# Memory projections in halves of 256 columns: the key half of both token tiles first, then the value half

## The reference, cut to what matters

```python
def memory_attention(q, mem, mem_norm_g, w_mem_kv, q_norm_g, k_norm_g):
    kv = rms_norm(mem, mem_norm_g) @ w_mem_kv            # (256, 1024) @ (1024, 512)
    k, v = jnp.split(kv.reshape(B, M, 2 * MEM_HEADS, HEAD_DIM), 2, axis=2)
    q = rms_norm(q, q_norm_g)
    k = rms_norm(k, k_norm_g)
    logits = jnp.einsum('bshd,bmhd->bhsm', q, k).astype(jnp.float32) * (HEAD_DIM ** -0.5)
    p = jax.nn.softmax(logits, axis=-1)
    out = jnp.einsum('bhsm,bmhd->bshd', p.astype(v.dtype), v)

for i in range(DEPTH):                                   # DEPTH = 2
    if i == 1: k_shared, v_shared = ...                  # from h @ w_kv
    h = swiglu_half_step(h, ffn1_norm[i], ffn1_w_gate_up[i], ffn1_w_down[i])
    z = rms_norm(h, mix_norm[i]) @ w_in[i]               # 1024 -> 1024
    y_mix = pool mixer (i = 0) or banded attention (i = 1) of z[..., :768]
    y_mem = memory_attention(z[..., 768:], mem, ...)
    h = h + concatenate([y_mix, y_mem]) @ w_out[i]
    h = swiglu_half_step(h, ffn2_norm[i], ffn2_w_gate_up[i], ffn2_w_down[i])
```

## Time and profile before

| | us |
|---|---|
| time, median of 3 runs | 980.77 (980.74 to 981.02) |
| span of the profiled execution, first to last instruction | 977.7 |
| PE busy | 949.3 (97%) |
| DVE busy | 554.0 (57%) |
| ACT busy | 457.7 (47%) |
| POOL busy | 50.0 (5%) |
| DMA queue of the weights | 164.65 MB, 50.6% of 16 engines' span |

### The profile page before, as it was taken

The page is one execution under the profiler, slowest core; times in us unless marked ns, Lnnn a source line. Parts: engine busy times, 40 slices in busy tenths (PEclk is TensorE's granted clock), DMA queues, the critical chain, the costliest instruction groups (busy, mean ns, idle before and its releaser), DMA issues.

```text
span 977.7 us, 12400 instructions
## 1 busy us (share of the span) xinstructions
PE 949.3 (97%) x4515; PEld 779.0 (80%) x4515; DVE 554.0 (57%) x650; ACT 457.7 (47%) x642; POOL 50.0 (5%) x85
## 2 busy tenths in 40 slices
PE   7999999999999999999899999999998999999998
PEld 5888888887777888888688888888876878888886
DVE  5655454674557455555676546455776565455552
ACT  6544444444435443444545434353556455353441
POOL 3300000010000000000210000000130000000000
PEclk9999999999999999999999999999999999999999
DMA  9966556364145746464366555652740246646442
GB/s 318 293 220 202 184 183 203 129 237 161 42 150 193 250 149 212 157 214 172 108 215 215 187 199 173 213 169 103 266 129 1 86 164 212 217 152 209 163 129 86
DMA packets 121054, 172.74 MB, mean 177 GB/s; under 512 B 5649, under 2 KB 95921, under 8 KB 121025
## 3 DMA queue, kind: packets, MB, share of 16 engines
q1 hardware_dynamic: 118416, 164.65, 50.6%
q0 software_dynamic: 2464, 7.64, 2.4%
q10 hardware_dynamic: 144, 0.07, 0.0%
HBM read 171.28 MB, written 1.05 MB: 176 GB/s over the span
## 4 chain that ended last, share of the span: by engine, by line
PE 90%; DVE 5%; ACT 2%; DMA 1%; issue 1%; POOL 1%; SPq 0%; POOLq 0%; DVEq 0%; ACTq 0%
PE ps L1042 19%; PE ps L1044 19%; PE ps L1043 19%; PE ps L1114 8%; PE ps L1116 8%; PE ps L1118 8%; PE ps L1097 2%; DVE w_lo L712 2%; PE ps L1034 1%; DMA w_raw<-in_ffn_w_gate_up_dram 1%; DVE mainT_lo L738 1%; ACT squares L489 1%; DVE xn L729 1%; PE ps L1180 1%; PE ps L1216 1%
## 5 line engine op out<-in xcount | busy, mean ns | idle before, releaser
L712 DVE TENSOR_TENSOR w_lo<-w_raw,w_hi 128x1024 fp32r<-128x1024 f32 x308 | 371.0, 1224 | 154.8 <-ACT w_hi L469 147.8
L469 ACT CAST w_hi<-w_raw 128x1024 fp32r<-128x1024 f32 x308 | 317.1, 1052 | 145.5 <-PE ps L1118 71.3
L1042 PE MATMUL ps<-w_hi,mainT_hi 128*128 128x512 f32 x832 | 329.8, 396 | 6.9 <-DVE w_lo L712 3.0
L1044 PE MATMUL ps<-w_hi,mainT_lo 128*128 128x512 f32 x832 | 324.7, 390 | 0.0
L1043 PE MATMUL ps<-w_lo,mainT_hi 128*128 128x512 f32 x832 | 324.1, 390 | 0.0
L1042 PEld LDWEIGHTS ps<-w_hi,mainT_hi 128*128 128x128 f32 x832 | 156.2, 188 | 42.3 <-issue 9.0
L1044 PEld LDWEIGHTS ps<-w_hi,mainT_lo 128*128 128x128 f32 x832 | 156.2, 188 | 33.3
L1043 PEld LDWEIGHTS ps<-w_lo,mainT_hi 128*128 128x128 f32 x832 | 156.4, 188 | 30.9
L505 ACT ACTIVATE silu_g<-ps 128x256 f32<-128x256 f32 x88 | 33.8, 384 | 234.3 <-PE ps L1044 234.1
L745 DVE TENSOR_TENSOR act_f<-ps,silu_g 128x256 f32<-128x256 f32 x88 | 37.3, 424 | 169.6 <-PE ps L1097 128.6
L1114 PE MATMUL ps<-w_hi,actT_hi 128*128 128x512 f32 x352 | 109.3, 392 | 0.3
(11 more groups left out here) (153 smaller groups left out, 530.0 us busy)
## 6 DMA issues: line engine op xcount, KB each, us to landing
w_raw<-in_ffn_w_gate_up_dram SPq DMA_DIRECT2D x176, 512.0 KB, 4.6
w_raw<-in_ffn_w_down_dram SPq DMA_DIRECT2D x88, 512.0 KB, 4.1
w_raw<-in_w_in_dram SPq DMA_DIRECT2D x16, 512.0 KB, 6.2
w_raw<-in_w_out_dram SPq DMA_DIRECT2D x16, 512.0 KB, 5.2
w_raw<-in_w_mem_kv_dram SPq DMA_DIRECT2D x8, 512.0 KB, 4.0
gain<-in_ffn_norm_dram POOLq DMA_DIRECT2D x4, 512.0 KB, 6.3
w_raw<-in_w_kv_dram SPq DMA_DIRECT2D x4, 512.0 KB, 4.0
h<-in_x_dram SPq DMA_DIRECT2D x2, 512.0 KB, 4.2
```

The source lines that it names most:

```text
L469: nc.scalar.copy(half(w_hi[s], b), half(w_raw[s], b)).then_inc(hi_ready[s], 1)
L712: nc.vector.tensor_tensor(half(w_lo[s], b), half(w_raw[s], b), half(w_hi[s], b).bitcast(F32), ALU.subtract).then_inc(lo_ready[s], 1)
L1042: pe.matmul(dst, x_hi, wh, start=start, stop=False)
L1044: return pe.matmul(dst, x_lo, wh, start=False, stop=stop)
```

## The change

The function `projection` is no longer used for `mkv0` and `mkv1`. A new function `mem_projection` computes four pieces in this order: keys (columns 0 to 255) of tile 0, keys of tile 1, values (columns 256 to 511) of tile 0, values of tile 1. Each piece is 24 matmuls of 256 moving columns and has a PSUM bank of its own (banks 4 and 5 for the keys, 6 and 7 for the values; before, two banks of 512). The weights of both slots are released only in the last piece. DVE copies the key pieces where `kv_copy` stood; the copy of the value pieces stands behind `head_norm("mk0")` in layer 0 and directly behind the key copies in layer 1. The wait for the copies in layer 0 is moved ahead of the transposes of the memory keys, which write banks 6 and 7.

```diff
+            def mkv_copy(part, base, name):
+                cols = slice(part * 256, part * 256 + 256)
+                for t in range(NT):
+                    if part == 1 and t == 1:
+                        dve.wait_ge(weights_used[slot(UNIT[name] + 1)], cycle(UNIT[name] + 1) * 2 + 2)
+                    else:
+                        dve.wait_ge(mkv_done, base // 4 * 3 + 2 * part + t + 1)
+                    nc.vector.tensor_copy(mkv_sb[:, t, cols], ps[:, GU_BANK + 2 * part + t, 0:256]).then_inc(mkv_ready, 1)
+                dve.wait_ge(mkv_ready, base + 2 * part + NT)
@@ DVE, layer 0 and layer 1
-            kv_copy(mkv_sb, mkv_done, mkv_ready, 0, "mkv0")
+            mkv_copy(0, 0, "mkv0")
             split("N2", 0, "main")
             split("N2", 1, "main")
             head_norm("mk0")
+            mkv_copy(1, 0, "mkv0")
...
-            kv_copy(mkv_sb, mkv_done, mkv_ready, NT, "mkv1")
+            mkv_copy(0, 4, "mkv1")
+            mkv_copy(1, 4, "mkv1")
             split("N7", 0, "main")
@@ PE
+            def mem_projection(name, split_name):
+                u = UNIT[name]
+                for part in range(2):
+                    cols = slice(part * 256, part * 256 + 256)
+                    for t in range(NT):
+                        for k in range(KC):
+                            s, kk = slot(u + k // 4), k % 4
...
+                            mm = three(ps[:, GU_BANK + 2 * part + t, 0:256],
+                                       tr_hi["side"][:, k, t * P:(t + 1) * P], tr_lo["side"][:, k, t * P:(t + 1) * P],
+                                       w_hi[s][:, kk, cols], w_lo[s][:, kk, cols], k == 0, k == KC - 1)
+                            if part == 1 and t == NT - 1 and kk % 2 == 1:
+                                mm.then_inc(weights_used[s], 1)
+                        if part == 0 or t == 0:
+                            mm.then_inc(mkv_done, 1)
...
-            projection("mkv0", "side", "N1", to_gu, mkv_done, lambda n: True)
+            mem_projection("mkv0", "N1")
             turn_norm(2)
...
             projection(*z0, blocks=(0,))
+            pe.wait_ge(mkv_ready, 4)
             turn_heads(0)
             projection(*z0, blocks=(1,), tiles=(0,))
             pe.wait_ge(consts_landed, 16 * SMALL_LOADS)
             pe.wait_ge(z_ready, NT)
-            pe.wait_ge(mkv_ready, NT)
...
-            projection("mkv1", "side", "N6", to_gu, mkv_done, lambda n: True)
+            mem_projection("mkv1", "N6")
```

More of the change, by code:

```diff
@@ L1076, in projection @@
                             mm.then_inc(done, 1)
+            def mem_projection(name, split_name):
[5 more added lines that the diff above has]
+                            s, kk = slot(u + k // 4), k % 4
+                            if part == 0 and k % 4 == 0:
+                                pe.wait_ge(split_lo, split_index(split_name, t, k // 4) + 1)
+                            if part == 0 and t == 0 and kk % 2 == 0:
+                                pe.wait_ge(lo_ready[s], cycle(u + k // 4) * 2 + (kk // 2 + 1))
+                            mm = three(ps[:, GU_BANK + 2 * part + t, 0:256],
[5 more added lines that the diff above has]
+                            mm.then_inc(mkv_done, 1)
             def ffn(f, norm, mem_norm=None):
@@ L1312, in _ @@
             projection(*z1, blocks=(0,))
-            pe.wait_ge(mkv_ready, 2 * NT)
+            pe.wait_ge(mkv_ready, 8)
             projection(*z1, blocks=(1,), tiles=(0,))
```

## The result

The changed kernel takes 987.50 us (median of 3 runs, 986.54 to 988.95) against 980.77 before: ratio 1.0069, 95% interval 1.0049 to 1.0088, some 6.7 us slower. Forecast were 984.7 and a range up to 987.5, which the median just reaches: the sign was right, and 2.8 us were not forecast. The profiled execution has a span of 987.0 us against 977.7, 9.3 more; it is the longest of the three changed ones. The times of the three lie 1.8 to 2.5 us above their spans. In all its later executions the kernel before has 1.75 to 1.86 there, not the 3.0 to 3.3 that I read off ahead of the prediction; its profiled execution was probably some 1.3 us shorter than the three timed ones, whose spans are not on record.

What follows compares the result with a forecast made beforehand. PE, busy 97% of the span with 90% of the chain, was taken as the bound, DVE from mainT_lo on in layer 1. +1.57 and +2.35 us made +3.9 on 980.77: 984.7 us, range 982.0 to 987.5.

Steps and rivals of the forecast that it cites:

- pace of 256 columns: Memory projections on PE: 120 ns per product of 256 columns, bounds 113.3 to 191 ns.
- pace and old order, both layers: PE's own cost of 96 shorter products per projection: +0.64 us in each layer, +1.3 in both.
- first cast after the projection's start: ACT's cast of the second z unit waits for the later weight release: 9.61 us instead of 7.05.
- layer 0, z later by: Late release and key copies delay mainT_lo on DVE, so PE starts z 1.57 us later.
- layer 1, z later by: Late release and all four copies ahead of mainT_lo on DVE: z 2.35 us later.
- value copies ahead of z in layer 1: Two value copies on DVE directly behind the key copies, ahead of mainT_lo: 0.79 us with their gaps.
- value copies behind the head norm in layer 0: Two copies on DVE, 0.79 us, covered by 2 us before PE needs the later low parts: nothing.
- second half of z in layer 1: PE's wait of 0.94 us there neither grows nor goes, as DVE's chain keeps its length.
- C: Clock gives back what the waits cost: shifted stages escape both half-clock stretches, 3.4 us; +0.5, 981.3 us; chance 0.05.
- D: Clock falls once more: new waits before z bring half clock into dense products, +1.7, 986.4 us; chance 0.06.
- A: Weight loads and products on PE take turns, 191 ns a product: about +15, 995.6 us; chance 0.07.
- B: Waiting before z is swallowed, casts and low parts off the path; only PE's 1.3 us remain, 982.1; chance 0.10.

Runs made afterwards that it cites:

- d1: Kernel before with 256-column products in old order, old release and 512-column copies, PE's idle time filled with zero products: 979.30 us.
- d3: Changed kernel with PE filled, layer 1 value copies moved behind the low parts PE waits for: 981.10 us.
- b2: Changed kernel with PE's idle time filled with bf16 products of zeros: 981.73 us.
- b1: Kernel before with PE's idle time filled with bf16 products of zeros at five places: 978.38 us, ratio 0.9935 to the kernel before.
- d4: Kernel before with the zero-product filling at the start alone: 983.67 us, ratio 1.0002.
- a1: The changed kernel run again, unfilled, against the kernel before: 988.05 us, ratio 1.0049.
- a2: Kernel before with 256-column products only, old order, old release and 512-column copies, unfilled: 988.25 us, ratio 1.0043.
- a4: Changed kernel, unfilled, key copies between low parts of z's first two units, layer 1 value copies behind later low parts: 984.75 us, ratio 1.0019.
- a3: Kernel before with 512-column products kept and only the late release of the weight slots, unfilled: 986.95 us, ratio 1.0039.
- d2: Kernel before with 512-column products and only the late weight release, PE's idle time filled: 980.92 us.
- b4: Changed kernel with DVE's copies moved off the path and PE's idle time filled: 979.13 us.

## Why the prediction was right in its terms and short in its sum

| step | forecast | measured |
|---|---|---|
| pace of 256 columns | 120 ns | 119.9 |
| pace and old order, both layers | +1.3 | +1.28 in the trace (2 x 0.64), +1.43 in time (d1) |
| first cast after the projection's start | 9.61 | 9.61 |
| layer 0, z later by | 1.57 | 1.54 |
| layer 1, z later by | 2.35 | 2.33 |
| value copies ahead of z in layer 1 | 0.79 | 0.79 in the trace (15.33 - 14.54), 0.77 in time (d3) |
| value copies behind the head norm in layer 0 | 0 | 0 (z to Y0 44.88 in b2, 44.87 in b1) |
| second half of z in layer 1 | unchanged | z1 to Y1 58.25 in b2, 58.24 in b1 |
| sum | +3.9 | +3.87 in the traces, +3.91 in time at full clock (b2 against b1) |

**The step that failed** is the term that the sum put at nothing: that outside the two stages both kernels take the same time, at the same clock, so that 3.9 can be added to the median of three executions. In its place the runs show 2.8 us more. I had the clock as rivals C and D, at 0.05 and 0.06, each worth one or two stretches of 3.4 us, and wrote against the one that "three runs lay within 0.3 us", as if the kernel before kept to one pattern of clock. It does not. Over the three groups the kernel before has 92 executions from 979.65 to 992.22 us; 61 lie at 983.32 or below, and 31 at 985.54 or above. Three that agree can come from one group of such a distribution. The stretches at 0.50 last 3.4 us in the trace that I read, but 6.8, 10, 13.7 and 17 in others; they fall at the start and at 260, 485, 707 and 740 us as the execution has it. The one of 13.7 us in d4 alone costs 6.2 us (64.46 against 58.24 from z1 to Y1). The range was built from one pattern.

The difference first measured, 6.7 us, is then 3.9 of schedule and 2.8 of the rest. Of the 5.4 us that the profiled executions differ by outside the two stages, 3.9 go with the clock and 1.5 are a late load. The execution of 987.50 us has no profile; its 2.8 us can't be split in the same way. But some 0.7 of them lie outside the span from first to last instruction (987.50 - 985.0 = 2.5, against 1.8 in the later executions of the kernel before). This recurs: a1, a2 and a4 have 1.85 to 3.03 us there, a3 and everything filled 1.76 to 1.91. It comes with products of 256 columns, and only where PE is not filled; its cause is open. The interval of a1, 3.0 to 6.6, includes 3.9.

In the first group the versions that start z later met half clock more often than the kernel before (the counts behind a4). One group shows it, and why they do is open. Both unfilled profiles of the changed kernel have a stretch at about 707 us, behind the longer wait of 1.91 us, where no other kernel's profile has one. But it costs little there (58.66 us from z1 to Y1 after the change, against 58.25 in b2 at full clock), b2's profile has none, and a3, with nearly the same wait, has none either.

**The rivals.** A (191 ns a product) is out by the pace. B is out by d2 and by the traces. C of the prediction (the clock gives back what the waits cost) came in part: the changed kernel's profile has no stretch at 736.6, but one at 708.5 and longer ones elsewhere. Its price of 3.4 us was too high, and 1.1 of it had no row: at full clock the span of the kernel before is 975.5 (b1) against 977.7, 2.2 less. D happened in kind, a stretch right behind the new wait, but it cost 0.4 us and not 1.7; what cost time were stretches at places that the change doesn't touch. The Trainium skill, "TensorE: Matmul & The Clock Gate", section "Back-to-back issue gap", gives N / 2.4 + 2.5 ns as the isolated gap of a warm product, 109 ns for 256 columns. That is not met: the trace has 119.9. The chances of the prediction do not add up either: its five cases make 1.00 and leave nothing for the 0.03 of "faster", and B and C alone, 0.15, are more than the 0.14 of "same".

## What to carry to other kernels

When products are reordered, ask first where the buffers that they read are counted free. Here the order of the pieces kept both weight slots busy until the last quarter, and everything behind them in the lists of two other engines moved with them; the columns per product cost less (1.3 us alone, against 3.1 for the late release alone). Read a term from the distance between two starts in the trace, and take a base time from more than three executions when PE stands still for some us anywhere: the clock can add more than the change. To compare two schedules, fill those gaps in both; and compare them unfilled too, since a change of schedule may come with a change in how often the clock falls.

## What the runs showed of the hardware

- A stream of fp32r products with a load of 128 columns for each goes at 226.7 ns for 512 columns and 119.9 for 256: 106.8 ns per 256 columns and 13.1 per product.
- bf16 products of zeros hold PE's clock up. With 44 more of them over five places (9, 6, 5, 14 and 10) the executions of the kernel before shrink from a spread of 12 us to one of 1.2, and the fastest gains 2.3 us (979.65 to 977.35).
- A stretch at 1.2 GHz in attention lasted 13.7 us (d4) and 17 (a2) although PE was busy in nearly all of it (13.70 of 13.70, 16.27 of 17.00), with transposes and small f32 products; it began during a wait of PE of 2.83 us or 1.3 us after its end.
- One and the same program met half clock for different lengths in different executions: mean granted clocks of 0.994 down to 0.979 in the 92 of the kernel before. In the first group 26 of its 35 were at 0.990 or above, against 17 of 48 of the four versions that start z later.
- The first load of the gain row let DVE begin at 7.53 us (b4) to 9.42 us (the changed kernel), a difference of 1.9 us between profiles at a place that none of the edits to the two stages touches.
